# Five of twelve modulation parts moved from TensorE's steps to VectorE's row products, in a two-layer transformer kernel on one core

## The reference

```
cond = silu(c)
for l in range(2):
    mod = cond @ w_ada[l] + b_ada[l]            # 1024 x 6144 -> 6144
    sh1, sc1, g1, sh2, sc2, g2 = split(mod, 6)  # parts 0..5
    h = layer_norm(x) * (1 + sc1) + sh1
    mix = mixer(h, w_in[l], ...)                # two kinds of attention, two gates, w_out
    x = layer_norm(ALPHA * x + g1 * mix, ln1_g[l], ln1_b[l])
    h = layer_norm(x) * (1 + sc2) + sh2
    x = layer_norm(ALPHA * x + g2 * moe(h), ln2_g[l], ln2_b[l])
# a second block of two layers follows; it doesn't read c
```

## Time and profile before

| | |
|---|---|
| median of 3 runs | 1751.49 us (1751.21 to 1754.15) |
| span of the profiled execution | 1750.7 us |
| TensorE busy | 1688.2 us, 96% |
| VectorE busy | 1212.5 us, 69% |
| ScalarE busy | 941.3 us, 54% |
| GpSimd busy | 238.9 us, 14% |

### The profile page before, as it was taken

One profiled execution on the slowest core, in us unless ns is written; L12 is line 12 of the kernel. 1 busy time (PEld: TensorE's weight loads), 2 busy tenths in 40 slices (PEclk: granted clock), 3 DMA queues, 4 the chain that ended last, 5 costly groups with the idle time before them and its releaser, 6 DMA issues.

```text
span 1750.7 us, 24913 instructions
## 1 busy us (share of the span) xinstructions
PE 1688.2 (96%) x10220; PEld 1428.5 (82%) x10220; DVE 1212.5 (69%) x1372; ACT 941.3 (54%) x1067; POOL 238.9 (14%) x209
## 2 busy tenths in 40 slices
PE   6999998999899999999989999999999999999999
PEld 3887885888689897788867889878888899978887
DVE  2547668899965867899987575575666656656664
ACT  4435545877644555688755463454436655445442
POOL 0420020000025002000005502000001710210000
PEclk9999998999999998999999999999999999999999
DMA  9975587999846236699947435456654634536551
GB/s 363 353 268 193 194 315 253 365 373 375 317 149 213 97 123 242 249 379 376 342 145 253 144 121 181 166 183 216 211 174 181 216 121 145 180 133 217 193 192 73
DMA packets 190912, 393.13 MB, mean 225 GB/s; under 512 B 6128, under 2 KB 110576, under 8 KB 174928
## 3 DMA queue, kind: packets, MB, share of 16 engines
q1 hardware_dynamic: 188384, 381.71, 62.1%
q0 software_dynamic: 1712, 7.50, 1.2%
q10 hardware_dynamic: 704, 2.33, 0.4%
HBM read 390.46 MB, written 1.05 MB: 224 GB/s over the span
## 4 chain that ended last, share of the span: by engine, by line
PE 80%; DVE 6%; issue 4%; POOL 4%; ACT 4%; DMA 1%; POOLq 0%; SPq 0%; DVEq 0%; ACTq 0%
PE ps L586 19%; PE ps L588 18%; PE ps L587 18%; PE ps L646 6%; PE ps L647 3%; PE ps L718 2%; DVE low L2022 2%; ACT whi L1413 2%; POOL TB L2963 1%; PE ps L737 1%; PE ps L920 1%; PE ps L888 1%; PE ps L903 1%; PE ps L650 1%; DMA AR<-in_w_ada 1%
## 5 line engine op out<-in xcount | busy, mean ns | idle before, releaser
L2022 DVE TENSOR_TENSOR low<-raw,whi 128x2048 fp32r<-128x2048 f32 x310 | 711.8, 2304 | 294.0 <-ACT whi L1413 291.9
L1413 ACT ACTIVATE whi<-raw 128x2048 fp32r<-128x2048 f32 x310 | 590.9, 1913 | 273.1 <-PE ps L588 202.0
L586 PE MATMUL ps<-HH,whi 128*128 128x256 f32 x960 | 275.6, 287 | 0.0
L587 PE MATMUL ps<-HH,whi 128*128 128x256 f32 x960 | 271.5, 283 | 0.0
L588 PE MATMUL ps<-HH,low 128*128 128x256 f32 x960 | 271.4, 283 | 0.0
L586 PE MATMUL ps<-whi,HH 128*128 128x512 f32 (+1 forms) x640 | 247.9, 387 | 17.7 <-DVE low L2022 7.4
L587 PE MATMUL ps<-low,HH 128*128 128x512 f32 (+1 forms) x640 | 243.6, 381 | 0.0
L588 PE MATMUL ps<-whi,HH 128*128 128x512 f32 (+1 forms) x640 | 243.5, 381 | 0.0
L586 PEld LDWEIGHTS ps<-HH,whi 128*128 128x128 f32 x960 | 183.9, 192 | 13.6 <-issue 13.6
L587 PEld LDWEIGHTS ps<-HH,whi 128*128 128x128 f32 x960 | 184.0, 192 | 0.0
L588 PEld LDWEIGHTS ps<-HH,low 128*128 128x128 f32 x960 | 183.9, 192 | 0.0
(11 more groups left out here) (349 smaller groups left out, 2571.3 us busy)
## 6 DMA issues: line engine op xcount, KB each, us to landing
raw<-in_w_gu SPq DMA_DIRECT2D x80, 1024.0 KB, 5.1
raw<-in_w_ff SPq DMA_DIRECT2D x66, 1024.0 KB, 5.0
raw<-in_w_in SPq DMA_DIRECT2D x58, 1024.0 KB, 5.3
raw<-in_w_d SPq DMA_DIRECT2D x40, 1024.0 KB, 5.0
raw<-in_w_gate SPq DMA_DIRECT2D x32, 1024.0 KB, 5.4
ada<-in_w_ada SPq DMA_DIRECT2D x16, 1024.0 KB, 7.1
raw<-in_w_out SPq DMA_DIRECT2D x16, 1024.0 KB, 5.0
AR<-in_w_ada SPq DMA_DIRECT2D x13, 1024.0 KB, 9.0
```

What stands on the lines that cost most here:

```text
L586: pe.matmul(out, lhs[0], rhs[0], start=start, stop=False)
L587: pe.matmul(out, lhs[0], rhs[1], start=False, stop=False)
L1413: act.activation(wide(i, whi), wide(i, raw), ACT.Copy).then_inc(*up("w_hi", i))
L2022: dve.tensor_tensor(wide(i, low), wide(i, raw), wide(i, whi).bitcast(F32), ALU.subtract).then_inc(*up("w_lo", i))
```

## The change

Five of the twelve parts, (layer, part) = (0, 4), (0, 3), (0, 5), (1, 1), (1, 0), are no longer made by steps and sums. For them the host lays w_ada out with the output channel on the partitions (`w_ada_t`): a chunk n is 128 channels x 1024 rows, 512 KB, and eight chunks make a part. silu(c) is broadcast to all partitions once (`c_row`, loaded over ScalarE's queue at the start, made by ScalarE behind the second lift). VectorE's `row_dot(n)` multiplies a chunk by c_row and sums along the row in one instruction, whose sum is the chunk's column of modT; `row_fin` adds b_ada for a part at once. The forty dots stand at places of VectorE's program (`ROW_TAKEN`, by `row_turn`); SP loads the chunks two or three at a time (`load_rows`) into ten places of 1024 columns. Steps 12 to 31 and sums 6 to 15 go. c_row lies where the second block's small rows lie, so these rows are loaded later, by GpSimd, behind the last dot. ScalarE waits for dot 21 before its copies of gates 0 and 4, since chunks lie in G; SP waits for dot 39 before it loads step 34.

```
-MOD_PLACES = ["qa", "vd1", "vd2"] + [f"qk{i}" for i in range(6)] + [f"at{i}" for i in range(10)] + ["pa", "out", "xT", "rt"]
-MOD_TAKEN = [{"qa": (8, 9)} | {place: (10 + i,) for i, place in enumerate(MOD_PLACES[1:22])}
-             | {"x1": (31, 32, 33), "rt": (34, 35), "ff": (36, 37, 38, 39, 40)},
+MOD_TAKEN = [{"qa": (8, 9), "vd1": (10,), "vd2": (11,), "x1": (32, 33), "rt": (34, 35), "ff": (36, 37, 38, 39, 40)},
...
+MOD_SUMMED = [{"vd2": (4,), "qk1": (5,), "moe": (16, 17), "ff": (18,)},
...
+ROW_PARTS = [(0, 4), (0, 3), (0, 5), (1, 1), (1, 0)]
+ROW_TAKEN = (("ka", 2), ("q0", 1), ("q1", 1), ("vd", 2), ("vd1", 2), ("vd2", 2), ("qk0", 2), ("qk1", 2), ("qk2", 2), ("qk3", 2),
+             ("qk4", 2), ("qk5", 2), ("at3", 2), ("at4", 3), ("at5", 3), ("at6", 2), ("at7", 2), ("pb0", 1), ("pb1", 1),
+             ("wsum", 1), ("pa0", 1), ("pa1", 1), ("pa2", 1))
+ROW_PLACES = (0, 1, 2, 3) * 2 + (4, 5, 0, 1, 2, 3) * 2 + (4, 5) + (0, 1, 6, 7, 8, 9) * 3
...
+        row_buffers = [z[:, 1024 * i:1024 * i + 1024] for z in (ada, G0, G1, AR0, AR1) for i in range(2)]
...
+        def load_rows(eng, *chunks):
+            for n in chunks:
...
+                if n in row_after:
+                    eng.wait_ge(*at("row_dot", row_after[n]))
+                eng.dma_start(row_slot[n], dr["w_ada_t"][n // 8, n % 8]).then_inc(*up(f"row{n % 6}", n, by=16))
...
+            for name, chunks in ((("qa", 1), (0, 1)), (("ka",), (2, 3)), (("vd", 0), (4, 5)), (("vd12", 0), (6, 7)), (("qk", 0), (8, 9)),
+                                 (("qk", 1), (10, 11)), (("qk", 2), (12, 13)), (("qk", 3), (14, 15)), (("qk", 4), (16, 17)),
+                                 (("qk", 5), (18, 19)), (("gate", GATE_ORDER[0]), (20, 21))):
                 load(number["A", 0, *name] + 7)
-                load_mod(sp, s)
+                load_rows(sp, *chunks)
+            load(number["A", 0, "gate", GATE_ORDER[2]] + 7)
+            load_rows(sp, 22, 23)
...
+            for name, chunks in ((("gate", GATE_ORDER[4]), (28, 29)), (("gate", GATE_ORDER[5]), (30, 31, 32)),
+                                 (("gate", GATE_ORDER[6]), (33, 34)), (("gate", GATE_ORDER[7]), (35, 36)), (("pb",), (37, 38, 39))):
+                load(number["A", 0, *name] + 7)
+                load_rows(sp, *chunks)
...
+                    act.activation(c_row, c_row, ACT.Silu).then_inc(*up("c_row"))
...
+            def row_dot(n):
...
+                dve.wait_ge(*at(f"row{n % 6}", n))
+                dve.scalar_tensor_tensor(out=w, in0=w, scalar=1.0, in1=c_row, op0=ALU.mult, op1=ALU.mult, accum_out=modT[:, a:a + 1]
+                                         ).then_inc(*up("row_dot", n))
...
                 for i in range(6):
                     taken("A", l, "qk", i)
                     if i % 3 == 1:
                         leave_bank(AR[:, 512 * i:512 * i + 512], ("qk", l, i), "pj_d", "qk", l, i)
                     mod_turn(l, f"qk{i}")
+                    row_turn(l, f"qk{i}")
                 if l == 0:
                     dve.wait_ge(*at("alibi_in"))
...
                 def next_gate(g):
                     taken("A", l, "gate", GATE_ORDER[g])
+                    row_turn(l, f"at{g}")
...
                     if m % 2:
-                        mod_turn(l, f"at{8 + m // 2}")
+                        row_turn(l, f"pb{m // 2}")
...
-                mod_turn(l, "pa")
+                row_turn(l, "wsum")
                 for m in range(4):
...
                     if m % 2:
                         taken("A", l, "pa", m // 2)
-                mod_turn(l, "out")
+                    row_turn(l, f"pa{m}")
```

More of the change, by code:

```diff
@@ L395, in build @@
         G0, G1, AR0, AR1 = G[:, 0:2048], G[:, 2048:4096], AR[:, 0:2048], AR[:, 2048:4096]
[L396 to L401, removed]
+        mod_slot = dict(enumerate([TB, G0, G1, AR0, AR1, AR[:, 4096:6144], T2, ada, TB, AR1, G1, AR0]))
+        mod_slot |= dict(enumerate([Bf[0], Bf[1], ada, Bf[0], ada, AR0, AR1, AR[:, 4096:6144], ada, AR0, ada, G0, ada, Bf[0], Bf[1], ada], 32))
+        mod_after = {s: max(r for r in mod_slot if r < s and mod_slot[r] is mod_slot[s])
+                     for s in mod_slot if any(mod_slot[r] is mod_slot[s] for r in mod_slot if r < s)}
         def mod_acc(j):
@@ L406, in mod_acc_after @@
         def mod_acc_after(j):
-            return [i for i in range(j) if (i in (1, 3, 16, 18, 20)) == (j in (1, 3, 16, 18, 20))][-1:]
+            return [i for i in (*range(6), *range(16, j)) if i < j and (i in (1, 3, 16, 18, 20)) == (j in (1, 3, 16, 18, 20))][-1:]
+        c_row = rows[:, ROWS_2:ROWS_2 + D]
+        row_buffers = [z[:, 1024 * i:1024 * i + 1024] for z in (ada, G0, G1, AR0, AR1) for i in range(2)]
+        row_slot = [row_buffers[i] for i in ROW_PLACES]
+        row_after = {n: max(r for r in range(n) if ROW_PLACES[r] == ROW_PLACES[n])
+                     for n in range(1, 40) if ROW_PLACES[n] in ROW_PLACES[:n]}
         def mod_half(s):
@@ L414, in mod_at @@
         def mod_at(l, part):
+            if (l, part) in ROW_PARTS:
+                return at("mod_part", l, part)
             return at("mod_cols", 2 * MOD_PARTS.index((l, part)) + 1)
@@ L529, in program_sp @@
             load(number["A", 0, "out", 3] + 7)
+            sp.wait_ge(*at("row_dot", 39))
             for s in (34, 35, 36):
@@ L2044, in mod_turn, with row_fin, row_turn @@
                     mod_fin(j)
+            def row_dot(n):
+                l, part = ROW_PARTS[n // 8]
+                a = 48 * l + 8 * part + n % 8
+                w = row_slot[n]
+                if n == 0:
+                    dve.wait_ge(*at("c_row"))
+                dve.wait_ge(*at(f"row{n % 6}", n))
+                dve.scalar_tensor_tensor(out=w, in0=w, scalar=1.0, in1=c_row, op0=ALU.mult, op1=ALU.mult, accum_out=modT[:, a:a + 1]
+                                         ).then_inc(*up("row_dot", n))
+            def row_fin(l, part):
+                a = 48 * l + 8 * part
+                o = modc(l, part)
+                dve.wait_ge(*at("row_dot", 8 * ROW_PARTS.index((l, part)) + 7))
+                if part in (1, 4):
+                    step(dve.tensor_tensor(o, o, col("b_ada", a, 8), ALU.add))
+                    dve.tensor_scalar(o, o, 1.0, None, ALU.add).then_inc(*up("mod_part", l, part))
+                else:
+                    dve.tensor_tensor(o, o, col("b_ada", a, 8), ALU.add).then_inc(*up("mod_part", l, part))
+            def row_turn(l, place):
+                if l == 0 and place in ROW_FROM:
+                    for n in range(ROW_FROM[place], ROW_FROM[place] + dict(ROW_TAKEN)[place]):
+                        row_dot(n)
+                        if n % 8 == 0 and n:
+                            row_fin(*ROW_PARTS[n // 8 - 1])
+                        if n == 39:
+                            row_fin(*ROW_PARTS[4])
             def ln_factors(sid, t):
@@ L2904, in first_block @@
                 roots(l, "out", sid)
+                if l == 0:
+                    pool.wait_ge(*at("row_dot", 39))
+                    pool.dma_start(rows[:, ROWS_2:N_ROWS], dr["rows"][ROWS_2:N_ROWS].partition_broadcast(P)).then_inc(*up("rows2_in", by=16))
                 norm_weights(l, "ff", "ln2_g", "ln2_b", T2[:, :], "H_lo", "S", l, 3)
@@ L3038 @@
     ff1 = a["w_ffn_in_2"].reshape(L, D, 2, FF // S, S).transpose(0, 1, 3, 2, 4).reshape(L, D, 2 * FF)
+    ada_t = a["w_ada"].reshape(L, D, 6, 8, P).transpose(0, 2, 3, 4, 1)
+    ada_t = np.stack([ada_t[l, part] for l, part in ROW_PARTS])
     arrays = {
         "x": a["x"][0], "mem": a["mem_2"][0], "cols": cols, "rows": rows, "na_b": na,
-        "w_ada": a["w_ada"], "w_in": a["w_in"], "w_pa": a["w_branch_a"], "w_pb": a["w_branch_b"],
+        "w_ada": a["w_ada"], "w_ada_t": ada_t, "c": a["c"].reshape(-1), "w_in": a["w_in"], "w_pa": a["w_branch_a"], "w_pb": a["w_branch_b"],
         "w_out": a["w_out"], "ln1_g": a["ln1_g"], "ln1_b": a["ln1_b"], "ln2_g": a["ln2_g"], "ln2_b": a["ln2_b"],
```

50 lines of the change are left out of this document (29 added, 21 removed).

## The result

| | before | after |
|---|---|---|
| median of the runs, us | 1752.59 (4 runs, 1751.21 to 1754.15) | 1765.02 (4 runs, 1763.56 to 1765.33) |
| span of the profiled execution, us | 1750.7 | 1761.8 |

The ratio is 1.0069, its 95% interval 1.0055 to 1.0083. The change makes the kernel 12.4 us slower by the medians, 11.1 us by the two profiled executions. The forecast was 1764 us, with 1763.6 for the span. The steps behind that sum are another matter: a stop for GpSimd was missing, the term for the start isn't on the path, and the term for the clock in the projection is absent from the profiled execution. That execution is the fastest of the changed kernel's four (1763.56 us, mean granted clock 0.977; the others 1764.8 to 1765.3 us, 0.973 to 0.975).

What follows compares the result with a forecast made beforehand. TensorE bound the kernel, VectorE from the late chunks to the projection after the change. +1.4 (start) +12.5 (to the projection's end) +2.5 (clock) -3.5 (router) = +12.9 us: 1764 us, eight in ten within 1749 to 1786.

Steps and rivals of the forecast that it cites:

- the term for the start: Start: c_row's 512 KB in ScalarE's queue, with all DMA engines full, delay the w_ada parts by 1.4 us.
- the term for the clock in the projection: Projection: TensorE's repeated idle times of 2 to 3 us lower its clock, +2.5 us, with 0 and 6 as ends.
- price of a dot: VectorE: a dot takes 1.20 us in a row of them, accumulation adding nothing.
- (b): First scores: after TensorE's idle time its clock is low for five microseconds, half of them lost, +2.5 us.
- router: Router's stretch: steps and sums taken off the chain of waits, -3.5 us.
- step (c): Behind gate 0: chunks 20 and 21 are issued late, VectorE's first biases wait, +13.0 us at the first turned copy.
- VectorE sets the time from there to the projection: Up to pa's first product: fifteen dots fill VectorE, which sets the time at 236.8 us; TensorE could be there before 232.
- Dots between the merges: Merges: the last three dots each stand in front of the next product, on the path, 3.6 us.
- rival 2: VectorE: accumulation halves its rate, 2.3 us a dot, 1791 us in all; chance 0.08.
- step (a): Before the first scores: late chunks hold VectorE's copy that frees qk,4 until 120.8 us; TensorE stands still for 4.1 us.
- Rival 3: First scores and projection: the clock stays low for 12 us at both, +3.5 us each, 1771 us; chance 0.10.
- Rival 4: Whole kernel: stalls are shorter than said and the sum ends near nothing, 1748 to 1755 us; chance 0.08.

Runs made afterwards that it cites:

- experiment 2: Changed kernel with dots 4 to 17 working on 8 of their 1024 columns, queue and waits kept: 1763.02 us, ratio 1.0066 to the kernel before.
- experiment 6: Changed kernel with c_row's load just ahead of the second lift instead of at the start: 1765.02 us, ratio 1.0072 to the kernel before.
- experiment 1: Changed kernel with chunks 20 and 21 issued with 18 and 19, not behind gate 0's fetch: 1751.58 us, ratio 0.9996 to the kernel before.
- experiment 3: Changed kernel with dots 37 to 39 behind the fourth merge instead of between the merges: 1761.86 us, ratio 1.0059 to the kernel before.
- experiment 4: Changed kernel with dots 22 to 39 working on 8 of their 1024 columns: 1754.35 us, ratio 1.0012 to the kernel before.
- experiment 9: Changed kernel with chunks 20 and 21 issued early and dots 22 to 39 on 8 of 1024 columns: 1740.14 us, ratio 0.9933 to the kernel before.
- experiment 10: Changed kernel with chunks 20 and 21 issued early and dots 34 to 39 behind the last merge: 1749.24 us, ratio 0.9979 to the kernel before.
- experiment 7: Changed kernel with chunks 20 and 21 early, dots 37 to 39 behind the merges and c_row late: 1749.30 us, ratio 0.9980 to the kernel before.

## Why the prediction was right, and where it wasn't

| step of the prediction | forecast | measured |
|---|---|---|
| price of a dot, in a row of them | 1.20 us | 1.15 us (1.22 long) |
| qk,4's copy, ahead of the first scores | 120.8 | 123.57; 121.32 in experiment 2 |
| first scores' wait on TensorE | 4.1 us, for VectorE | 8.5 us, for GpSimd |
| low clock behind it, (b) | +2.5 us | +1.4 (transposes 1.98 for 1.02, scores 3.38 for 2.92); +2.6 in experiment 6 |
| gate 0 ends | 132.2 | 135.3 (its fetch) |
| last dot (21) ahead of the biases ends | 141.4 | 144.1 |
| first turned copy | 157.0 | 159.4 |
| low part of 188.46 | 198.5 | 201.0 |
| first product of pa | 236.8 | 238.1 |
| last low part of the merges ends | 257.3 | 258.6 |
| clock in the projection | +2.5 us | nothing in the profiled execution; +2.1 in experiment 6's |
| start | +1.4 | +1.3 there, nothing from 67 us on |
| router | -3.5 | -4.4 |

The forecast's points leave out the 1.4 us of the start, which its sum adds by itself. With them the first product of pa is at 238.2 and the last low part ends at 258.7 us, within 0.1 us of the measured ones. That is luck: the start isn't on the path, and its 1.4 us stand in for what GpSimd added.

**Right: step (c), the queue's order.** Chunks 20 and 21 behind gate 0's fetch cost +13.0 us at the first turned copy by the forecast. Experiment 1 removes exactly this: 13.3 us come off at the first turned copy (146.15 for 159.42), 11.7 at the last merge and 13.4 in the median.

**Right: VectorE sets the time from there to the projection.** 34.90 us of 34.93 busy, and experiments 3, 4, 9 and 10 each move it by dots. Dots between the merges: 3.6 us forecast, 3.5 measured at the last merge; experiment 3 shows that 1.1 of them reach x(1).

**Right: the price, and against rival 2.** The Trainium skill (Vector Engine (DVE) Microarchitecture Reference, "Points that are easy to get wrong") has this form at half throughput; forty dots of 1.22 us, against 1.28 without accumulation, say that it doesn't hold here. The measurement decides.

**Mis-sized: step (a), and why.** The prediction costed VectorE's new work by VectorE alone and never asked what it does to GpSimd. The profile of before had the answer in it: GpSimd's 128x256 instructions took 0.75 us or 2.8, by whether VectorE was at a low part. In the changed kernel the rotation ends 23.6 us later: it starts 4.4 us later, behind the norm that stands behind the first dots, and takes 19.2 us more beside a full VectorE. The wait became 8.5 us instead of 4.1, and all points behind it are 1.3 to 3.1 us later than forecast. As VectorE was close behind (experiment 2), the mistake is worth 1.8 us at gate 0 by these two traces: the scores start 3.8 us earlier in experiment 2, and the low clock takes 2.0 of them back. The low clock of (b) is there (granted 0.58 from 122 to 128 us; the scores take 5.33 us in experiment 2, 3.38 in the changed kernel, 2.92 in the earlier trace rows), and again from 138 to 154 us at 0.50, in a stretch where the chain runs through VectorE. Rival 3, low for 12 us at the scores and in the projection, didn't come: at these two places it is low for about 6 us (121 to 127) and 5 us (242 to 247), and for some 9 and 8 us in experiment 6's trace.

**Mis-sized: the start.** The +1.4 us are right where they were read (the step that waited for its part until 18.12 now waits until 19.42) and wrong as a term of the sum. At qa's first product 0.9 us are left (38.04 for 37.18; 36.86 in experiment 6). The chain of the changed kernel leaves TensorE at the first chunk, which lands at 67.09 us, and goes on over VectorE and GpSimd to the first scores. What TensorE lost at the start is not on it. Experiments 6 and 7 take the term away, and the medians move by 0.0 and 0.1 us; their spread is wider than the term, but the traces agree from 67.09 to 123.57 us.

**Neither right nor wrong: the clock in the projection.** TensorE waited there as said (9.2 us), but in the profiled execution its granted clock is below 1 from 242 to 247 us only, at the start of the stretch, when it waits for VectorE anyway; then 1.00. So x(1)'s last step comes 13.4 us later than before (279.13 for 265.76), where the sum had 1.4 + 12.5 + 2.5 = 16.4. Experiment 6's trace has the term, with 2.1 us. The changed kernel's three other runs are slower than the profiled one at a lower mean clock; whether they have it too isn't known.

**Where the gain went.** TensorE has 26 us less to do. With the queue's wait and the late dots out of the way (experiment 9) 12.0 of them reach the median. Most of the other 14 is in that trace's waits of TensorE: 8.1 us for GpSimd ahead of ka's transposes, 2.3 for turned probabilities and 2.4 in the projection, 12.8 us where before has 0.2. The late dots take 11.4 back (experiments 9 and 1), and the queue's order 13.4 (experiment 1 and the changed kernel). That -12.0 + 11.4 + 13.4 give the whole loss is so by construction and confirms nothing; in the other order the queue is worth 14.2 (experiments 4 and 9) and the late dots 10.7.

**What the sum left out, and what stays open.** The difference is 13.4 us at x(1)'s last step and 9.0 at the experts' first products behind the router (290.47 for 281.46): the router gave back 4.4, not 3.5. From there the prediction had nothing changing, and no run was made for it, but the traces show where the difference grows again to 11.1 us. At 448.74 us (439.69 before) it is still 9.05; at 472.31 (461.66) it is 10.65. Between them the clock is low in the changed kernel and not before, though TensorE is busy without a gap in both (from 425 us on):
```profile
450.72:455.02 4.30, 4.30 (x12) 3.39 (x13) 4.24 (x5) 1.00 (x3) 0.00 (x0) 0.60 0.51 211
```
By 499 us the difference is 11.1, and behind that it moves between 9.7 and 11.1. Experiment 6's trace has no such dip between 425 and 465 us. So 1 or 2 us of a single trace's difference come from where the clock happens to fall; why it falls there no run shows. 1764 against 1765.0 is closer than its terms: too little for GpSimd and for what comes behind the router, too much for the start. Rival 4, a time of 1748 to 1755 us, is out by the measured time.

## What to carry to other kernels

Work moved to an engine that has time on average is paid in three places that the average doesn't show: the queue that loads its data (here one pair of chunks behind a wait for TensorE was worth 13.4 us), the engine beside it (GpSimd's rotation took 40.0 us instead of 20.9), and the stretch in which it was already half busy (11.4 us). Look at the queue's order first: two chunks issued one turn earlier turned +0.7% into nothing, and three dots moved made it -0.2%. And where two stops stand one behind the other, removing one shows the other, not its own price. A difference of 1 to 3 us between two traces can be the clock's: the same stretch of code took 21.3 and 23.3 us.

## What the runs showed of the hardware

- A scalar_tensor_tensor of 128x1024 float32, both inputs in SBUF, with its sum over the row: 1.22 us, one every 1.15 us in a row, with 0.08 us for the read of the accumulator hidden. Beside GpSimd it took up to 1.77 us.
- GpSimd's tensor_tensor of 128x64 float32: 0.33 us alone or beside VectorE's copy out of PSUM, 1.2 to 2.4 us beside VectorE's dots and low parts; one of 128x256: 0.75 us alone, up to 2.85. VectorE lost less by it: up to 0.55 us a dot, where GpSimd lost up to 2.1 us an instruction.
- TensorE's granted clock in two executions of the same stretch of code: 1.00 (changed kernel) and 0.52 (experiment 6) from 259 to 266 us; the stretch took 2.1 us longer. And it was 0.60 over 4.3 us of the changed kernel (450.72 to 455.02), though TensorE had been busy without a gap from 425 us on.
